# Feed-forward input of a hybrid decoder trunk: combinations of weight blocks made by adding DMAs

## The chip, the cores and the metric

The kernel runs on one core of one Trainium2 chip. The metric is the device time of one execution in microseconds (us); the median of three runs of the kernel before is 1497.92 us (1497.32 to 1499.15).

## What is computed

The reference is one layer of a decoder trunk for 256 tokens with a width of 2048, all in float32: three parallel token mixers with gates and an output projection, then a cross attention into 256 memory tokens, then a SwiGLU feed-forward. The change touches only the first half of the feed-forward:

```python
h = rms_norm(x, ffn_pre_gain[l])
gt, up = jnp.split(h @ w_ffn_in[l], 2, axis=-1)        # w_ffn_in: 2048 x 11264, FFN_HIDDEN = 5632
x = x + rms_norm((jax.nn.silu(gt) * up) @ w_ffn_out[l], ffn_post_gain[l])
```

## The kernel before, in words

**Weights in units.** All weights are streamed from HBM in units of 512 KB: 128 partitions x 1024 float32, that is two tiles of 128 x 512. A queue of the sync engine (SP in the profile) loads them into `raw`, a ring of four buffers. Every product is made of float32 numbers split into two parts: ScalarE (ACT) copies a unit into `w_hi` in the reduced type (line 547 in the feed-forward), VectorE (DVE) subtracts it from `raw` to give `w_lo` (line 995), and TensorE (PE) multiplies hi by hi, lo by hi and hi by lo. `w_hi` and `w_lo` are rings of four too. This pair of operations on one unit is called a split here. The split for step v waits for `unit_used >= v - 3`, that is until PE has finished step v - 4; it starts when PE begins step v - 3.

**Bodies.** The feed-forward input has 11 column groups of 512 gate columns (left, G) and 512 up columns (right, U). The first group is computed plainly. The other ten are ten bodies of 19 steps each, i = 1 to 10. In a body 12 steps are plain units (12 matmuls of 128 x 512 each), six for G and six for U. The remaining quarter of the sum is done by a Strassen-like scheme with seven block products (6 matmuls each) where a plain computation has eight. It takes a 2 x 2 arrangement of weight units B11, B12 (gate and up of one half of the rows) and B21, B22, and the same of the inputs. The weight sides of the seven products are, in this order, B11, B12 - B11, B22 - B12, B22 - B12 + B11, B22, B21 and B21 - (B22 - B12 + B11); the left-hand sides are sums of input blocks, `S_f`, formed once (`x_sums`, line 1600). The partial products go to the PSUM banks `side[2]`, `side[3]`, `tr[0]` and `tr[1]`, and DVE folds them into the two column groups afterwards (`sum_p6`, `sums_p7_p5`, `sum_p5`, `gate_sum`, `up_sum`).

**Who forms the combinations of weight blocks.** DVE does, in `difference` (line 1003): four subtractions per body, in place in `raw`, before the split of the combination. In the program the order of a body is fixed: six plain units, the seven block products one behind another, six plain units. Steps are numbered r0 to r18 below, and the four subtractions make the combinations of r7, r8, r9 and r12.

**The order on the other engines.** Everything is written out by hand. A Python function, `late_units`, makes the list of loads (which unit into which of the four buffers, and after how many splits that buffer is free) and the list of steps. SP walks the loads in order, each behind a wait for `lo_ready`, the count of finished splits. ACT and DVE walk the same steps four ahead of PE; at position j of body i they do the split of step j + 4 of that body. Between the splits stand the other tasks of the body, at fixed positions: on DVE `up_sum` and `hidden_product` of the body before (j = 0, 1), `hidden_turn` (j = 2, two 32 x 32 block transposes into `h_blk`), the partial sums (j = 13 to 16) and `hidden_lo` (j = 17); on ACT the copy of one partial product out of PSUM (line 928), `hidden_hi` (line 595) and Silu (line 934). GpSimd (POOL) issues 16 small DMAs of 32 KB per body (`spread_blocks`, line 502) once the transposes are done; they finish the transposition of the hidden activations, and `hidden_hi` waits for their landing.

The same scheme occurs six times in the second half of the feed-forward (`out_pair`); it keeps the DVE subtractions.

Of the kernel before, what the change touches and what calls it, by code (L numbers as in the profile page):

```python
# [40 lines left out]
RING = 4  # L41
# [23 lines left out]


def late_units():

    loads, steps = [], {}
    free, rounds = [S_FI - 3 + k for k in range(RING)], [S_FI // RING] * RING  # L70
    slot, pairs = 0, 0

    def load():
        nonlocal slot
        s, slot = slot, (slot + 1) % RING
        rounds[s] += 1
        loads.append((S_FI + len(loads), s, free[s]))
        return s, rounds[s] * 16

    def plain(count):  # L80
        for _ in range(count):
            s, landed = load()
            v = S_FI + len(steps)
            steps[v] = ("plain", 0, 0, (s,), (landed,))
            free[s] = v + 1

    def pair():
        nonlocal slot, pairs
        v = S_FI + len(steps)
        slots, landed = zip(*[load() for _ in range(4)])  # L90
        for k in range(7):
            steps[v + k] = ("pair", k, pairs, slots, landed)
        for s, done in zip(slots, (7, 3, 5, 6)):
            free[s] = v + done
        slot, pairs = (slot + 1) % RING, pairs + 1

    for _ in range(10):
        plain(6)
        pair()
        plain(6)  # L100
# [8 lines left out]
    assert len(steps) == S_END - S_FI  # L109
    return loads, steps  # L110


LATE_LOADS, LATE_STEPS = late_units()
B11, B12, B22, B21 = range(4)

# [41 lines left out]
def trunk(nc, units, x, x_t, mem, mem_t, columns, gm_ws_t, s5_b_t, s5_c_t, gm_v_gain,  # L157
          mix_post_gain, xattn_post_gain, ffn_post_gain, out):
    with ExitStack() as ctx:
# [138 lines left out]
        def bank(b, h):  # L298
# [44 lines left out]
        t_ready, p1_copied, u_part, u_done, silu_ready, hb_ready = (  # L343
            sem("t_ready"), sem("p1_copied"), sem("u_part"), sem("u_done"), sem("silu_ready"), sem("hb_ready"))
        hs_ready, hs_hi, hs_lo = sem("hs_ready"), sem("hs_hi"), sem("hs_lo")
        hT_turned, hT_hi_ready, hT_ready = sem("hT_turned"), sem("hT_hi_ready"), sem("hT_ready")
# [62 lines left out]
        def _(pool):  # L409
# [103 lines left out]
        def _(act):  # L513
# [22 lines left out]
            def split_late(v):  # L536

                if v >= S_END:
                    return
                kind, k, n, slots, landed = LATE_STEPS[v]  # L540
                block = 0 if kind == "plain" else (B11, B11, B12, B11, B22, B21, B11)[k]
                if kind == "plain" or k in (0, 4, 5):
# [377 lines left out]
            def ffn_in(i):  # L920
                for j in range(FI_SPLITS):
                    if j == 12:
                        act.wait_ge(unit_used, body_base(i) + 7)
                        if i == 1:
                            act.wait_ge(acc_taken[1], G_FI + 2)
                        else:
                            act.wait_ge(hb_ready, i - 1)
                        a_.activation(silu_g[:, 0], side[:, 2], ACT.Copy).then_inc(p1_copied, 1)
                    if j == 15:
                        hidden_hi(i)  # L930
                    if j == 17:
# [47 lines left out]
        def _(dve):  # L979
# [25 lines left out]
            def split_late(v):  # L1005
# [3 lines left out]
                kind, k, n, slots, landed = LATE_STEPS[v]  # L1009
                if kind == "plain":  # L1010
                    split_at(slots[0], v)
                    return
# [587 lines left out]
            def x_sums():  # L1600

                a = [[xg[:, h, 0].rearrange("p (q e) t -> p e q t", e=2)[:, e] for e in range(2)] for h in range(HALVES)]
                own.link(v_.tensor_tensor(S_f[:, 0], a[1][0], a[1][1], ALU.add))
                own.link(v_.tensor_tensor(S_f[:, 1], S_f[:, 0], a[0][0], ALU.subtract))
                v_.tensor_tensor(S_f[:, 2], a[0][0], a[1][0], ALU.subtract)
                v_.tensor_tensor(S_f[:, 3], a[0][1], S_f[:, 1], ALU.subtract).then_inc(s_ready, 1)

# [23 lines left out]
            def up_sum(i, h):  # L1631

                if h == 0:
                    dve.wait_ge(acc0_full, G_FI + 2 + i)
                else:
                    dve.wait_ge(unit_used, body_base(i + 1))
                v_.tensor_tensor(hb[:, h], bank(1, h), hb[:, h], ALU.add).then_inc(acc_taken[h], 1)

# [8 lines left out]
            def gate_sum(i, h):  # L1647

                dve.wait_ge(unit_used, body_base(i) + 12 + h)
# [8 lines left out]

            def sums_p7_p5(m, second, third):
# [4 lines left out]
                v_.tensor_tensor(second, side[:, 3], second, ALU.add).then_inc(u_part, 1)  # L1664

            def sum_p5(m, third, fourth):

                dve.wait_ge(u_part, 3 * m)
                v_.tensor_tensor(fourth, side[:, 3], third, ALU.add).then_inc(u_done, 1)

            def ffn_in(i):
                for j in range(FI_SPLITS):
# [10 lines left out]
                    if j == 2:  # L1683
                        hidden_turn(i)
                    if j == 13:
                        dve.wait_ge(unit_used, body_base(i) + 10)
                        dve.wait_ge(h_blocked, i)
                        sum_p6(i, silu_g[:, 0], hb[:, 0])
                    if j == 14:
                        sums_p7_p5(i, hb[:, 0], silu_g[:, 1])  # L1690
                    if j == 15:
                        sum_p5(i, silu_g[:, 1], hb[:, 1])
                        gate_sum(i, 0)
                    if j == 16:
                        gate_sum(i, 1)
                    if j == 17:
# [92 lines left out]
        def _(pe):  # L1789
# [307 lines left out]

            def pair_products(v, hi, lo, g, s_hi_, s_lo_, x12_free, first, last):
# [5 lines left out]
                if x12_free is not None:  # L2104
                    pe.wait_ge(acc_taken[0], x12_free)
                pair_product(v + 4, side[:, 0], *sum_of(s_hi_, s_lo_, 3), x12_free is not None, False)
                pair_product(v + 5, acc[:, 0], *block_of(hi, lo, g, 1, 0), False, x12_free is not None)
                pair_product(v + 6, acc[:, 1], *block_of(hi, lo, g, 1, 1), False, x12_free is not None)

# [35 lines left out]
            def out_pair(q, k, pair):  # L2145

                pe.wait_ge(hs_lo, k + 1)
                pe.wait_ge(u_done, 10 + pair)
                pair_products(S_FO + q, hT_hi, hT_lo, k, H_hi[k], H_lo[k], None, k == 0, k == PAIRED - 1)

# [119 lines left out]
```

## Time and profile before

| | |
|---|---|
| median of three runs | 1497.92 us |
| the profiled execution's own time | 1497.17 us |
| its span, first to last instruction | 1495.1 us |
| PE (TensorE) busy | 1483.7 us, 99% |
| DVE (VectorE) busy | 1129.9 us, 76% |
| ACT (ScalarE) busy | 825.7 us, 55% |
| POOL (GpSimd) busy | 151.9 us, 10% |
| mean granted TensorE clock | 0.998 |
| moved by DMA | 305.08 MB |
| ten bodies of the feed-forward input | from 834.06 us on, 42.16 us each |

The span is the time on the core's engines; the execution's own time has 2.1 us more around it. A busy engine is one with an instruction in flight. Matmul rows overlap: a row of 0.39 us stands every 0.227 us. The idle time of an engine costs something only where PE waits for it in turn.

### The profile page before, as it was taken

How to read it: one execution, taken by the hardware profiler on the slowest of the kernel's cores; microseconds unless marked ns; L12 is line 12 of the kernel's file. 1: busy time of each engine (PE TensorE's matmuls, PEld its weight loads, DVE VectorE, ACT ScalarE, POOL GpSimd, SP SyncE). 2: the span in 40 equal slices, each digit the busy share in tenths (PEclk: the TensorE clock that was granted, in tenths of full speed). 3: DMA queues.
4: the chain of work that ended last, by engine and by line, in shares of the span. 5: the costliest groups of instructions: out<-in, count | busy, mean ns of one | idle time of the engine just before them, and what ended most of it. 6: DMA issues, size and time to landing. Idle time of an engine off the chain costs nothing.

```text
span 1495.1 us, 19180 instructions
## 1 busy us (share of the span) xinstructions
PE 1483.7 (99%) x6718; PEld 1221.6 (82%) x6718; DVE 1129.9 (76%) x1346; ACT 825.7 (55%) x990; POOL 151.9 (10%) x286
## 2 busy tenths in 40 slices
PE   9999999999999999999999999999999999999997
PEld 7888887888888888888887888888888888888886
DVE  7878988855554577557577788888888888887786
ACT  7645445565666444556576455555555555555553
POOL 0000000140220000000000221112222221000000
PEclk9999999999999999999999999999999999999999
DMA  9755555666565655856453666766666667657554
GB/s 347 234 187 179 172 183 181 200 197 197 186 194 172 237 181 186 325 195 212 155 197 113 199 209 221 230 212 214 209 210 203 202 214 233 231 171 238 197 184 154
DMA packets 89858, 305.08 MB, mean 204 GB/s; under 512 B 13056, under 2 KB 13568, under 8 KB 88768
## 3 DMA queue, kind: packets, MB, share of 16 engines
q1 hardware_dynamic: 80144, 285.12, 57.4%
q0 software_dynamic: 9216, 18.63, 3.9%
q8 instruction: 41, 0.67, 0.2%
q10 hardware_dynamic: 432, 0.45, 0.1%
q14 instruction: 25, 0.20, 0.0%
HBM read 294.19 MB, written 2.10 MB: 198 GB/s over the span
## 4 chain that ended last, share of the span: by engine, by line
PE 97%; DVE 1%; DMA 1%; ACT 1%; issue 0%; DVEq 0%; POOL 0%; SPq 0%; ACTq 0%; POOLq 0%
PE acc L1803 10%; PE acc L1805 9%; PE acc L1804 9%; PE acc L2123 6%; PE acc L2124 6%; PE acc L2121 6%; PE side L2123 5%; PE side L2124 5%; PE side L2121 5%; PE side L1803 3%; PE side L1804 3%; PE side L1805 3%; PE tr L1805 3%; PE tr L1803 3%; PE tr L1804 3%; PE side L2085 1%
## 5 line engine op out<-in xcount | busy, mean ns | idle before, releaser
L547 ACT ACTIVATE w_hi<-raw 128x1024 fp32r<-128x1024 f32 x296 | 312.5, 1061 | 300.6 <-PE acc L2124 98.6
L990 DVE TENSOR_TENSOR w_lo<-raw,w_hi 128x1024 fp32r<-128x1024 f32 x262 | 320.9, 1227 | 202.0 <-ACT w_hi L528 197.7
L995 DVE TENSOR_TENSOR w_lo<-raw,w_hi 128x1024 fp32r<-128x1024 f32 x312 | 378.6, 1223 | 113.8 <-ACT w_hi L547 103.0
L528 ACT ACTIVATE w_hi<-raw 128x1024 fp32r<-128x1024 f32 x262 | 277.1, 1060 | 281.0 <-PE acc L1805 165.8
L1803 PE MATMUL acc<-w_hi,xT_hi 128*128 128x512 f32 x504 | 198.2, 393 | 0.0
L1805 PE MATMUL acc<-w_hi,xT_lo 128*128 128x512 f32 x504 | 196.3, 389 | 0.0
L1804 PE MATMUL acc<-w_lo,xT_hi 128*128 128x512 f32 x504 | 196.3, 389 | 0.0
L502 POOL DMA_DIRECT2D hT_st<-h_blk x176 | 93.9, 542 | 493.7 <-DVE h_blk L1062 455.3
L1803 PEld LDWEIGHTS acc<-w_hi,xT_hi 128*128 128x128 f32 x504 | 94.6, 188 | 21.5 <-issue 1.6
L1805 PEld LDWEIGHTS acc<-w_hi,xT_lo 128*128 128x128 f32 x504 | 94.6, 188 | 20.0
L1804 PEld LDWEIGHTS acc<-w_lo,xT_hi 128*128 128x128 f32 x504 | 94.7, 188 | 19.1
L2121 PE MATMUL acc<-w_hi,xT_hi 128*128 128x512 f32 x240 | 93.4, 389 | 0.0
L2123 PE MATMUL acc<-w_lo,xT_hi 128*128 128x512 f32 x240 | 93.4, 389 | 0.0
L2124 PE MATMUL acc<-w_hi,xT_lo 128*128 128x512 f32 x240 | 93.4, 389 | 0.0
L2121 PE MATMUL side<-w_hi,xT_hi 128*128 128x512 f32 x240 | 93.4, 389 | 0.0
L2123 PE MATMUL side<-w_lo,xT_hi 128*128 128x512 f32 x240 | 93.4, 389 | 0.0
L2124 PE MATMUL side<-w_hi,xT_lo 128*128 128x512 f32 x240 | 93.4, 389 | 0.0
L1003 DVE TENSOR_TENSOR raw<-raw 128x1024 f32<-128x1024 f32 x64 | 78.3, 1224 | 3.3 <-DMA raw<-in_units 0.6
L1803 PE MATMUL tr<-w_hi,xT_hi 128*128 128x512 f32 x192 | 75.8, 395 | 0.0
L1805 PE MATMUL tr<-w_hi,xT_lo 128*128 128x512 f32 x192 | 74.9, 390 | 0.0
L1804 PE MATMUL tr<-w_lo,xT_hi 128*128 128x512 f32 x192 | 74.8, 390 | 0.0
L1803 PE MATMUL side<-w_hi,xT_hi 128*128 128x512 f32 x160 | 62.7, 392 | 0.5 <-DVE w_lo L990 0.5
(467 smaller groups left out, 2743.2 us busy)
## 6 DMA issues: line engine op xcount, KB each, us to landing
raw<-in_units SPq DMA_DIRECT2D x530, 512.0 KB, 4.2
hT_st<-h_blk POOLq DMA_DIRECT2D x176, 32.0 KB, 2.1
x_tok<-in_x SPq DMA_DIRECT2D x4, 512.0 KB, 5.9
qkT<-qk_blk POOLq DMA_DIRECT2D x64, 32.0 KB, 2.6
xres<-in_x POOLq DMA_DIRECT2D x1, 2048.0 KB, 10.4
m_raw<-in_mem_t POOLq DMA_DIRECT2D x1, 2048.0 KB, 10.9
mq<-in_mem POOLq DMA_DIRECT2D x1, 2048.0 KB, 17.7
x_raw<-in_x_t SPq DMA_DIRECT2D x6, 256.0 KB, 5.9
```

The costliest lines, as they stand in the source:

```text
L502: g.dma_start(hT_st[32 * a:32 * a + 32, :, b].rearrange("p h k c -> p h (k c)"), h_blk[32 * b:32 * b + 32, :, a].rearrange("p h k c -> p h ...
L528: a_.activation(w_hi[:, j % RING], raw[:, j % RING], ACT.Copy).then_inc(hi_ready, 1)
L547: a_.activation(w_hi[:, v % RING], raw[:, slots[block]], ACT.Copy).then_inc(hi_ready, 1)
L990: v_.tensor_tensor(w_lo[:, s], raw[:, s], w_hi[:, s].bitcast(F32), ALU.subtract).then_inc(lo_ready, 1)
L995: v_.tensor_tensor(lo[:, v % RING], raw[:, slot], hi[:, v % RING].bitcast(F32), ALU.subtract).then_inc(lo_ready, 1)
L1003: v_.tensor_tensor(raw[:, dst], raw[:, minuend], raw[:, subtrahend], ALU.subtract).then_inc(t_ready, 1)
L1803: pe.matmul(bank(b, h), hi[:, kt, tok], w_hi[:, s, k], start=begin, stop=False)
L1804: pe.matmul(bank(b, h), hi[:, kt, tok], w_lo[:, s, k], start=False, stop=False)
L1805: mm = pe.matmul(bank(b, h), lo[:, kt, tok], w_hi[:, s, k], start=False, stop=end)
L2121: pe.matmul(bank(b, h), hi[:, kt, tok], whi[:, k], start=(j == 0 and k == 0 and begins[h] is not None), stop=False)
L2123: pe.matmul(bank(b, h), hi[:, kt, tok], wlo[:, k], start=False, stop=False)
L2124: mm = pe.matmul(bank(b, h), lo[:, kt, tok], whi[:, k], start=False, stop=(last and j == count - 1 and k == 1))
```

## The change

The four combinations of a body are no longer made by DVE. GpSimd issues DMAs that read a unit from HBM and add it to what lies in a buffer of `raw` (`accum_op=ALU.add`), four per body. Since a DMA adds only, the signs are moved: the inputs' block sums and the folding on DVE take other signs (`x_sums`, `up_sum`, `sums_p7_p5`, `sum_p5`), so that the weights' combinations are B22 + B12, B11 + B12, B22 + B12 + B11 and B22 + B12 + B11 + B21. B12 is no longer loaded by itself; it is read twice, by two adding DMAs. A body has 15 loads and 4 adding DMAs where it had 16 loads.

The order of the 19 steps changes: the seven products no longer stand together. Their steps are r2 (B22), r3 (B11), r6, r7, r10 (sums), r13 (B21) and r14 (sum), and in every case a DMA fills or adds to a buffer right behind the split four steps ahead of its next use. The number of matmuls is the same. The wait of PE for `u_done` of the body before and for the bank that the up columns leave (`acc_taken[0]`) move to r2; the latter stood ahead of r10 before.

```diff
+BODY = ("G0", "G1", "B22", "B11", "G2", "G3", "B22+B12", "B11+B12", "G4", "G5", "B22+B12+B11",
+        "U0", "U1", "B21", "B22+B12+B11+B21", "U2", "U3", "U4", "U5")
+SUMS = ("B22+B12", "B11+B12", "B22+B12+B11", "B22+B12+B11+B21")
...
+    def body(i):
+        nonlocal v, u
+        at = {}
+        for r, what in enumerate(BODY):
+            if "+" in what:
+                held, added = what.rsplit("+", 1)
+                slot, split = at[held]
+                sums.append((SUMS.index(what), slot, u + BODY_UNITS.index(added), split + 1))
+                steps[v + r] = ("sum", SUMS.index(what), i, (slot,), (16 * i,))
+            else:
+                longer = [k for k, w in enumerate(BODY) if w == what or w.startswith(what + "+")]
+                slot, landed = load(u + BODY_UNITS.index(what), v + longer[-1] + 1)
+                steps[v + r] = ("plain", 0, 0, (slot,), (landed,))
+            at[what] = slot, v + r
...
-            spread_blocks(1)
-            for i in range(2, 12):
+            def add_blocks(role, slot, u, splits):
+
+                pool.wait_ge(lo_ready, splits)
+                g.dma_start(raw[:, slot].rearrange("p a b -> p (a b)"), units[u], accum_op=ALU.add).then_inc(sum_landed[role], 16)
+
+            for i in range(1, 11):
+                for k in range(3):
+                    add_blocks(*LATE_SUMS[4 * (i - 1) + k])
                 spread_blocks(i)
+                add_blocks(*LATE_SUMS[4 * (i - 1) + 3])
+            spread_blocks(11)
...
+                if kind == "sum":
+                    act.wait_ge(sum_landed[k], landed[0])
...
-                    if j == 12:
-                        act.wait_ge(unit_used, body_base(i) + 7)
+                    if j == 5:
+                        act.wait_ge(unit_used, body_base(i) + 4)
...
-                    if j == 15:
+                    if j == 14:
                         hidden_hi(i)
...
             for i in range(1, 11):
                 v, taken = body_base(i), i * 2 + G_FI
-                plain_units(v, 6, 0, xT_hi, xT_lo, 4, (taken - 1, taken - 1))
+                plain_units(v, 2, 0, xT_hi, xT_lo, 4, (taken - 1, taken - 1))
                 if i == 1:
                     pe.wait_ge(s_lo, 1)
                 else:
                     pe.wait_ge(u_done, i - 1)
-                pair_products(v + 6, xT_hi, xT_lo, 0, S_hi, S_lo, taken, True, True)
-                plain_units(v + 13, 6, 1, xT_hi, xT_lo, 4, (None, taken), True)
+                pe.wait_ge(acc_taken[0], taken)
+                pair_product(v + 2, side[:, 0], *sum_of(S_hi, S_lo, 3), True, False)
+                pair_product(v + 3, side[:, 2], *block_of(xT_hi, xT_lo, 0, 0, 0), True, True)
+                plain_units(v + 4, 2, 0, xT_hi, xT_lo, 8)
+                pair_product(v + 6, tr[:, 0], *sum_of(S_hi, S_lo, 2), True, True)
+                pair_product(v + 7, side[:, 3], *sum_of(S_hi, S_lo, 0), True, True)
+                plain_units(v + 8, 2, 0, xT_hi, xT_lo, 12)
+                pair_product(v + 10, tr[:, 1], *sum_of(S_hi, S_lo, 1), True, True)
+                plain_units(v + 11, 2, 1, xT_hi, xT_lo, 4, (None, taken))
+                pair_product(v + 13, acc[:, 0], *block_of(xT_hi, xT_lo, 0, 1, 0), False, True)
+                pair_product(v + 14, acc[:, 1], *block_of(xT_hi, xT_lo, 0, 1, 1), False, True)
+                plain_units(v + 15, 4, 1, xT_hi, xT_lo, 8, last=True)
```

**GpSimd's queue.** The order on GpSimd from the start of the bodies, before. `hT_st<-h_blk` are the 16 small DMAs of a body.

```order
L494 DMA post_gain<-in_xattn_post_gain 128x2048 [waits acc1_taken,acc0_taken]
L502 DMA hT_st<-h_blk 32x2x128 [waits h_blocked]
L502 DMA hT_st<-h_blk 32x2x128 x15
L502 DMA hT_st<-h_blk 32x2x128 [waits hT_ready,h_blocked]
L502 DMA hT_st<-h_blk 32x2x128 x15
```

And the same place now; `raw<-in_units` is an adding DMA.

```order
L512 DMA post_gain<-in_xattn_post_gain 128x2048 [waits acc1_taken,acc0_taken]
L526 DMA raw<-in_units 128x1024 [waits lo_ready] x3
L520 DMA hT_st<-h_blk 32x2x128 [waits h_blocked]
L520 DMA hT_st<-h_blk 32x2x128 x15
L526 DMA raw<-in_units 128x1024 [waits lo_ready] x4
L520 DMA hT_st<-h_blk 32x2x128 [waits hT_ready,h_blocked]
L520 DMA hT_st<-h_blk 32x2x128 x15
```

Three adding DMAs stand ahead of the small DMAs of a body and the fourth behind them; the row of four is the fourth of body 1 and the first three of body 2.

**VectorE in a body.** The order on DVE in body 1 before, from the transposes of `hidden_turn` to the second of the partial sums. `w_lo<-raw,w_hi` is the DVE half of a split, `raw<-raw` a subtraction of weight blocks.

```order
L1062 STREAM_TRANSPOSE h_blk<-hb 128x4x4x32 x2
L995 TENSOR_TENSOR w_lo<-raw,w_hi 128x1024
L1003 TENSOR_TENSOR raw<-raw 128x1024 x2
L995 TENSOR_TENSOR w_lo<-raw,w_hi 128x1024
L1003 TENSOR_TENSOR raw<-raw 128x1024
L995 TENSOR_TENSOR w_lo<-raw,w_hi 128x1024 x3
L1003 TENSOR_TENSOR raw<-raw 128x1024
L995 TENSOR_TENSOR w_lo<-raw,w_hi 128x1024 x6
L1657 TENSOR_TENSOR hb<-tr,silu_g 128x512
L995 TENSOR_TENSOR w_lo<-raw,w_hi 128x1024
L1662 TENSOR_TENSOR silu_g<-tr,hb 128x512
```

And now:

```order
L1090 STREAM_TRANSPOSE h_blk<-hb 128x4x4x32 x2
L1023 TENSOR_TENSOR w_lo<-raw,w_hi 128x1024 x9
L1685 TENSOR_TENSOR hb<-tr,silu_g 128x512
L1023 TENSOR_TENSOR w_lo<-raw,w_hi 128x1024
L1690 TENSOR_TENSOR silu_g<-tr,hb 128x512
L1692 TENSOR_TENSOR hb<-hb,side 128x512
L1023 TENSOR_TENSOR w_lo<-raw,w_hi 128x1024
L1697 TENSOR_TENSOR hb<-silu_g,side 128x512
```

The four subtractions are gone. The partial sums begin two splits earlier: the first (`hb<-tr,silu_g`) stands between the splits of r14 and r15.

**ScalarE in a body.** The ACT halves of the splits from r6 on, in body 1, now; `sum_landed` is the landing of an adding DMA.

```order
L575 ACTIVATE w_hi<-raw 128x1024 [waits unit_used,sum_landed0]
L575 ACTIVATE w_hi<-raw 128x1024 [waits unit_used,sum_landed1]
L575 ACTIVATE w_hi<-raw 128x1024 [waits unit_used,w_landed0]
L956 ACTIVATE silu_g<-side 128x512 [waits acc1_taken,unit_used]
L575 ACTIVATE w_hi<-raw 128x1024 [waits unit_used,w_landed1]
L575 ACTIVATE w_hi<-raw 128x1024 [waits unit_used,sum_landed2]
L575 ACTIVATE w_hi<-raw 128x1024 [waits unit_used,w_landed3]
```

Before, the splits of combinations (r7, r8, r9 and r12) waited there for DVE's count `t_ready`; now those of r6, r7, r10 and r14 wait for a DMA.

## Rows read from the trace of the kernel before

**Rows 1.** The page: busy time, share of the span, instructions of two engines.

```profile
PE 1483.7 (99%) x6718; PEld 1221.6 (82%) x6718; DVE 1129.9 (76%) x1346; ACT 825.7 (55%) x990; POOL 151.9 (10%) x286
```

**Rows 2.** Waits of PE: who waited for whom, us in total, times, longest.

```profile
PE acc L2039 <- DVE xT_lo L1543: 1.4, 2, 1.3
PE side L1826 <- POOL warm L412: 1.4, 1, 1.4
PE side L1803 <- DVE w_lo L990: 0.5, 1, 0.5
```

**Rows 3.** Windows, one per body: length, busy us (x instructions), clock, DMA share.

```profile
core 0: us, PE busy (x) PEld busy (x) DVE busy (x) ACT busy (x) POOL busy (x), PEclk, DMA share, GB/s
876.22:918.38 42.16, 42.16 (x187) 34.91 (x186) 35.84 (x36) 22.74 (x23) 8.53 (x16) 1.00 0.66 208
918.38:960.54 42.16, 42.16 (x188) 34.91 (x186) 35.94 (x36) 22.74 (x23) 8.54 (x16) 1.00 0.70 218
```

**Rows 4.** Timeline of PE, body 3: start us, us, then what it is.

```profile
934.70 0.39 PE L2084 MATMUL side<-w_hi,xT_hi 128*128 128x512 f32 x1
...
936.06 0.39 PE L2084 MATMUL side<-w_hi,S_hi 128*128 128x512 f32 x1
...
944.22 0.39 PE L2121 MATMUL side<-w_hi,xT_hi 128*128 128x512 f32 x1
...
960.54 0.39 PE L2121 MATMUL acc<-w_hi,xT_hi 128*128 128x512 f32 x1
```

**Rows 5.** The subtractions of weight blocks in 886 to 1264 us: min/median/max ns.

```profile
L1003 DVE TENSOR_TENSOR raw<-raw x36: 1217/1225/1227, 887.0 to 1233.7; 128x1024 f32<-128x1024 f32 x36
```

**Rows 6.** Timeline of ACT at the start of body 4 (960.54 us).

```profile
960.80 1.06 ACT L547 ACTIVATE w_hi<-raw 128x1024 fp32r<-128x1024 f32 x1 [1.66 <-PE side L2124]
```

**Rows 7.** Timeline of DVE in bodies 3 and 4.

```profile
948.94 0.69 DVE L1657 TENSOR_TENSOR hb<-tr,silu_g 128x512 f32<-128x512 f32 x1
...
961.89 1.23 DVE L995 TENSOR_TENSOR w_lo<-raw,w_hi 128x1024 fp32r<-128x1024 f32 x1 [1.49 <-ACT w_hi L547]
963.03 1.28 DVE L1637 TENSOR_TENSOR hb<-side,hb 128x512 f32<-128x512 f32 x2
...
968.48 1.30 DVE L1062 STREAM_TRANSPOSE h_blk<-hb 128x512 f32<-128x512 f32 x2
970.05 1.22 DVE L995 TENSOR_TENSOR w_lo<-raw,w_hi 128x1024 fp32r<-128x1024 f32 x1 [0.28 <-ACT w_hi L547]
```

**Rows 8.** Timeline of DVE ahead of and in body 1 (starts at 834.06 us).

```profile
823.97 1.22 DVE L1611 TENSOR_TENSOR S_lo<-S_f,S_hi 128x1024 fp32r<-128x1024 f32 x1
...
836.55 1.40 DVE L1618 SCALAR_TENSOR_TENSOR hb<-side,rstd,silu_g 128x512 f32<-128x512 f32 x2
```

**Rows 9.** Timeline of POOL: the 16 small DMAs of bodies 2 and 3.

```profile
885.75 8.53 POOL L502 DMA_DIRECT2D hT_st<-h_blk  x16 [33.59 <-DVE h_blk L1062]
927.91 8.54 POOL L502 DMA_DIRECT2D hT_st<-h_blk  x16 [33.63 <-DVE h_blk L1062]
```

**Rows 10.** Timeline of POOL: issue of two DMAs of 512 KB.

```profile
33.83 0.69 POOL L429 DMA_DIRECT2D B_all<-in_s_b_t  x1 [30.67 <-DMA x_tok<-in_x]
34.52 0.53 POOL L430 DMA_DIRECT2D C_all<-in_s_c_t  x1
```

**Rows 11.** DMA queues in 886 to 1264 us: packets, MB, share of 16 engines.

```profile
q1 hardware_dynamic: 20690, 75.32, 60.5%
q0 software_dynamic: 4608, 4.73, 4.8%
raw<-in_units SPq DMA_DIRECT2D x144, 512.0 KB, 4.3
```

**Rows 12.** Unit loads in 886 to 1264 us, then small DMAs: landing, min/median/max.

```profile
DMA to landing us min/median/max: 3.0/4.3/6.5
...
DMA to landing us min/median/max: 1.7/2.1/4.9
```

**Rows 13.** DMA issues of GpSimd, whole kernel: count, KB, median us to landing.

```profile
post_gain<-in_xattn_post_gain POOLq DMA_DIRECT2D x1, 1024.0 KB, 7.0
post_gain<-in_ffn_post_gain POOLq DMA_DIRECT2D x1, 1024.0 KB, 7.6
B_all<-in_s_b_t POOLq DMA_DIRECT2D x1, 512.0 KB, 5.5
C_all<-in_s_c_t POOLq DMA_DIRECT2D x1, 512.0 KB, 7.7
```

More of the change, by code:

```diff
@@ L73, in load @@
-    def load():
-        nonlocal slot
-        s, slot = slot, (slot + 1) % RING
+    v, u, pairs = S_FI, S_FI, 0
+    def load(unit, done):
+        s = free.index(min(free))
         rounds[s] += 1
-        loads.append((S_FI + len(loads), s, free[s]))
+        loads.append((unit, s, free[s]))
+        free[s] = done
         return s, rounds[s] * 16
     def plain(count):
+        nonlocal v, u
         for _ in range(count):
-            s, landed = load()
-            v = S_FI + len(steps)
+            s, landed = load(u, v + 1)
@@ L84, in plain @@
             steps[v] = ("plain", 0, 0, (s,), (landed,))
-            free[s] = v + 1
+            v, u = v + 1, u + 1
     def pair():
-        nonlocal slot, pairs
-        v = S_FI + len(steps)
-        slots, landed = zip(*[load() for _ in range(4)])
+        nonlocal v, u, pairs
+        slots, landed = zip(*[load(u + k, v + done) for k, done in enumerate((7, 3, 5, 6))])
         for k in range(7):
             steps[v + k] = ("pair", k, pairs, slots, landed)
-        for s, done in zip(slots, (7, 3, 5, 6)):
-            free[s] = v + done
@@ L95, in pair @@
[L95 to L100, printed above, removed]
+        v, u, pairs = v + 7, u + 4, pairs + 1
+    def body(i):
+        nonlocal v, u
+        at = {}
[10 more added lines that the diff above has]
+            at[what] = slot, v + r
+        v, u = v + len(BODY), u + len(BODY_UNITS)
@@ L101, in late_units @@
+    for i in range(1, 11):
+        body(i)
     for count in (12, 8, 4):
@@ L108, in late_units @@
     plain(12)
-    assert len(steps) == S_END - S_FI
-    return loads, steps
-LATE_LOADS, LATE_STEPS = late_units()
+    assert v == S_END
+    return loads, steps, sums
+LATE_LOADS, LATE_STEPS, LATE_SUMS = late_units()
 B11, B12, B22, B21 = range(4)
@@ L344, in trunk @@
             sem("t_ready"), sem("p1_copied"), sem("u_part"), sem("u_done"), sem("silu_ready"), sem("hb_ready"))
+        sum_landed = [sem(f"sum_landed{i}") for i in range(4)]
         hs_ready, hs_hi, hs_lo = sem("hs_ready"), sem("hs_hi"), sem("hs_lo")
@@ L540, in split_late @@
                 kind, k, n, slots, landed = LATE_STEPS[v]
-                block = 0 if kind == "plain" else (B11, B11, B12, B11, B22, B21, B11)[k]
-                if kind == "plain" or k in (0, 4, 5):
+                block = 0 if kind != "pair" else (B11, B11, B12, B11, B22, B21, B11)[k]
+                if kind == "sum":
+                    act.wait_ge(sum_landed[k], landed[0])
+                elif kind == "plain" or k in (0, 4, 5):
                     act.wait_ge(w_landed[slots[block]], landed[block])
@@ L1009, in split_late @@
                 kind, k, n, slots, landed = LATE_STEPS[v]
-                if kind == "plain":
+                if kind != "pair":
                     split_at(slots[0], v)
@@ L1636, in up_sum @@
                     dve.wait_ge(unit_used, body_base(i + 1))
-                v_.tensor_tensor(hb[:, h], bank(1, h), hb[:, h], ALU.add).then_inc(acc_taken[h], 1)
+                v_.tensor_tensor(hb[:, h], bank(1, h), hb[:, h], ALU.subtract).then_inc(acc_taken[h], 1)
             def hidden_product(i):
@@ L1647, in gate_sum @@
             def gate_sum(i, h):
-                dve.wait_ge(unit_used, body_base(i) + 12 + h)
+                dve.wait_ge(unit_used, body_base(i) + 14 + h)
                 if h == 1:
@@ L1657, in sum_p6, with sums_p7_p5 @@
                 v_.tensor_tensor(second, tr[:, 1], first, ALU.add).then_inc(u_part, 1)
-            def sums_p7_p5(m, second, third):
+            def sums_p7_p5(m, second, third, op=ALU.add):
                 dve.wait_ge(u_part, 3 * m - 2)
@@ L1663, in sums_p7_p5, with sum_p5 @@
                 dve.wait_ge(u_part, 3 * m - 1)
-                v_.tensor_tensor(second, side[:, 3], second, ALU.add).then_inc(u_part, 1)
-            def sum_p5(m, third, fourth):
+                v_.tensor_tensor(second, second, side[:, 3], op).then_inc(u_part, 1)
+            def sum_p5(m, third, fourth, op=ALU.add):
                 dve.wait_ge(u_part, 3 * m)
-                v_.tensor_tensor(fourth, side[:, 3], third, ALU.add).then_inc(u_done, 1)
+                v_.tensor_tensor(fourth, third, side[:, 3], op).then_inc(u_done, 1)
             def ffn_in(i):
@@ L2096, in sum_of, with pair_products @@
                 return (lambda q: hi[:, m, q]), (lambda q: lo[:, m, q])
-            def pair_products(v, hi, lo, g, s_hi_, s_lo_, x12_free, first, last):
+            def pair_products(v, hi, lo, g, s_hi_, s_lo_, first, last):
                 pair_product(v, side[:, 2], *block_of(hi, lo, g, 0, 0), first, last)
```

38 lines of the change are left out of this document (18 added, 20 removed).

## The prediction, made before the changed kernel was run

> **What bounds the kernel now.** I read four views, from the whole to one body. The page first: PE has an instruction in flight for 1483.7 of 1495.1 us [rows 1]. Then the waits of PE: three in the whole kernel, 3.3 us together, and none of them on a weight combination [rows 2]. Then windows cut at the bodies: 42.16 us each, PE busy for all of it at a granted clock of 1.00 (the level of 2.4 GHz), DVE for 35.9 us, GpSimd for 8.5 us [rows 3]. Last the timeline of PE in body 3: from the first block product at 934.70 us to the next plain unit at 944.22 us are 42 matmuls, 9.52 us or 0.2267 us each; the product of 6 takes 936.06 - 934.70 = 1.36 us [rows 4]. A body has 12 x 12 + 7 x 6 = 186 matmuls, and 186 x 0.2267 = 42.16 us, the window's length to the last digit. So nothing is lost in a body: PE issues at its pace through the subtractions of DVE, and whatever ACT, DVE and the DMAs do lies beside it.
>
> **What the change removes.** Four subtractions of 1.225 us per body [rows 5], 4.9 us, 49 us over ten bodies. By the above they are hidden in full: worth 0 us. DVE's idle time in a body grows from 6.3 to about 11 us. The matmuls are as many as before and in the same shapes, so a body can't be shorter than 42.16 us. The change can only add waits, and the question is whether the adding DMAs are in time.
>
> **The timetable.** In us from the start of a body, with 2.72 for a plain unit and 1.36 for a product, the new steps start on PE at: r0 0, r1 2.72, r2 5.44, r3 6.80, r4 8.16, r5 10.88, r6 13.60, r7 14.96, r8 16.32, r9 19.04, r10 21.76, r11 23.12, r12 25.84, r13 28.56, r14 29.92, r15 31.28, r16 34.00, r17 36.72, r18 39.44, next body 42.16. A split starts when PE begins the step three earlier: ACT at 960.80 for a body that begins at 960.54, +0.26 [rows 6]; DVE begins at 961.89 and its result is there at 963.12, +2.6 [rows 7]. From a landing to the end of the split that waited for it are about 1.0 + 1.3 = 2.3 us. D is the time of an adding DMA from its issue to its landing.
>
> - r2 to r6: the split of r2 is done at -0.1. The add for r6 must be there by 13.60 - 2.3 = 11.3: D up to 11.4.
> - r3 to r7: issued at 2.6, needed by 12.7: D up to 10.
> - r6 to r10: its split comes behind the transposes on DVE, which end at 969.78, or 9.3 into the body, and the split of one more unit ends at 971.27, or 10.7 [rows 7]. Needed by 19.5: D up to 8.8.
> - r10 to r14: here GpSimd's order counts. The third add is issued at 10.7 and holds GpSimd for 0.5 to 0.7 us [rows 10]; the 16 small DMAs behind it take 8.54 us [rows 9]; so the fourth add, whose split would be ready at 17.6, is issued only at 19.9. DVE has the first partial sum (0.69 us [rows 7]) between the splits of r14 and r15, so r14's split has to be done by 31.28 - 0.7 - 1.2 = 29.4. D up to 29.4 - 2.3 - 19.9 = 7.2. This is the tightest place.
>
> Beyond these single limits there is a loop from body to body, in which each of three adds waits for the one before: from PE's start of r15 to that of r18 8.16, the split of the next r2 2.6, three times D + 2.3, the partial sum and the split of r15 1.9; together 19.6 + 3 D, against 42.16: D up to 7.5. So below some 7.2 us an add costs nothing, and above about 7.4 each us of D costs 3 us per body, 30 us in all.
>
> **How long is an adding DMA?** The trace has none; it is bounded by its neighbours. From below: a plain load of a unit lands after 4.3 us in the median, 3.0 at the least [rows 12]. From above: a DMA that GpSimd issues with twice the bytes takes 7.0 and 7.6 us, and the second of two 512 KB DMAs at once 7.7 us [rows 13]. I take 5.9: the fixed part by a small DMA of GpSimd, 2.1 [rows 12], then the transfer. 144 loads took 60.5% of 378 us, 1.6 us of all 16 engines each [rows 11]; an add has two streams of 512 KB to read, the unit and the buffer, so I take twice that, 3.2. A load needs 0.6 us more in the median than 2.1 + 1.6, for what shares the engines with it, and I give the add the same. That is 1.3 us under the tightest limit, so no wait: 0 us.
>
> The Trainium skill bears on the factor of two (Collectives: The Full Stack, "The bandwidth ceiling: the fold count and why AG ≠ RS ≠ AR"): the add inside a DMA costs nothing by itself, but the two source reads go through one ring and halve the rate, 32.35 against 62.28 GB/s. No row here shows it. By that page an add would be an estimated 1.93 x 1.6 = 3.1 us of transfer; by a plain copy's rate it would be 1.6. Both keep the sum at 0 us.
>
> **The DMA engines and the ring.** Per body 15 loads x 1.6 = 24.0, four adds x 3.2 = 12.8, small DMAs 4.8% of 42.16 = 2.0 us: 38.8 of 42.16, or 92%, where it was 65%. The order helps: behind each split exactly one DMA starts, a load or an add, so they come one after the other every 1.36 to 2.72 us and don't bunch. Each buffer's content is used four steps after the DMA began; 19 steps of 42.16 us allow 8.9 us per four steps, less the split's 2.3: all DMAs together may take 6.6 us in the mean. With loads at 4.3 and adds at 5.9 the mean is 4.6; with loads at 6 it would still hold.
>
> **The moved waits.** PE now waits at r2 for the bank that `up_sum` frees: DVE does its first half by 963.7, 3.2 into the body [rows 7], and r2 starts at 5.44; 2.2 us to spare. In body 1 that is the product at 836.55 plus 0.7, or 3.2 into it, as much to spare; and `S_lo` is there at 825.2, r2 starts at 839.5 [rows 8]. The small DMAs start 1.9 us later (11.4 instead of 9.5) and land at about 22; `hidden_hi` wants them at 31.5, the split behind which it stands. No cost. GpSimd has 4 x 0.6 us more to issue, in 33.6 us of idle time [rows 9]. Outside the ten bodies nothing moves.
>
> **The sum.** The profiled execution's own time is 1497.17 us, 2.1 more than its span, and 0.75 below the median of the runs. Minus 0, plus 0: the changed kernel takes the median's 1497.92, rounded 1498.0.
>
> **The rivals.**
> 1. *The adding DMA is slower than 7.4 us, and each body waits for it* (slower). For it: the same bytes from GpSimd took 7.7 us once, in company [rows 13]; the rate of an add is shown nowhere; three of four adds hang on one another, so a small excess is tripled. Against: 7.7 was the second of two issued together, here they come singly, except after r2 and r3. At 7.7 us it is 3 x 0.3 x 10 = 9 us, 1507; at 8.5 us 3 x 1.1 x 10 = 33 us, 1531. It decides from 7.4 us on. PE would wait at r14 and r15, for a split behind `sum_landed3`. Chance 24%.
> 2. *The DMA engines fill up* (slower). The adds take more of the engines than two streams, or the loads beside them stretch past the ring's 6.6 us. If loads and adds take 7.2 in the mean, 19/4 x 0.6 = 2.9 us per body, 29 in all, 1527. For it: 92% is close to full, and single loads take 6.5 already [rows 12]. Against: the spacing. Chance 12%.
> 3. *Faster by more than 0.2%.* It would need a loss in the bodies that the trace of before doesn't show. PE's waits there are zero and its pace doesn't depend on DVE's load. Chance 4%.
> 4. No change, the forecast: 60%.
>
> **How the numbers follow.** 0.2% (3 us) is what a measurement of this kernel can tell from no change. Within it lies the forecast, 60%; the likeliest case's own range is 1495 to 1501. Slower: rivals 1 and 2, 36%. Faster: 4%. The range goes up to 1531, where both slower cases as priced end; the tail above it, an add of over 8.5 us, holds some 15%. Below it ends at 1495.
>
> **What would show it.** Right: bodies of 42.16 us in the windows, no wait of PE on `w_lo` in them; ACT's copies for r6 and r10 start later than PE lets them, since the adds land after that (for r10 the slack without any shift is 15.2 - 10.7 = 4.5 us, less than D), and still PE doesn't wait; DVE at about 31 us per body. Adds of 5 to 7 us, loads of 4.3 to 5.5. Wrong: bodies over 42.5 us with PE waiting for DVE's split at r14 or r15 and ACT for a DMA before it (rival 1); or ACT waiting for plain loads and DMA engines over 90% busy (rival 2).

## The result, and the profile after

The changed kernel takes 1508.93 us (median of 4 runs, 1504.47 to 1511.67) against 1497.81 us: a ratio of 1.0073, 95% interval 1.0061 to 1.0084. It is slower by 11 us. The forecast of no change, given 60%, was wrong. The range held the time, but by the room it left for the rivals and not by the sum. The first rival, given 24%, comes nearest: PE waits at r14 for a split behind an adding DMA that is slower than 7.4 us. But only the fourth add of a body is slow, and not every body waits. The profiled execution took 1511.67 us; its span is 1509.9 us, 14.8 longer than before.

First the page's line of the engines, which answers to [rows 1], and the waits of PE, which answer to [rows 2] (who waited for whom, us in total, times, longest).

```profile
PE 1490.6 (99%) x6718; PEld 1222.5 (81%) x6718; DVE 1081.3 (72%) x1306; ACT 824.3 (55%) x990; POOL 187.7 (12%) x326
...
PE acc L2111 <- DVE w_lo L1023: 6.6, 5, 3.1
```

DVE has 49 us less to do, as worked out; PE has as many matmuls and is busy 7 us longer. A wait has appeared that is not in [rows 2]: the product on `acc` (r14) waits for DVE's half of a split. Windows cut at PE's start of r14 in one body and the next answer to [rows 3]; the columns are those of [rows 3].

```profile
864.22:907.62 43.40, 42.81 (x187) 34.76 (x186) 31.09 (x33) 22.51 (x24) 12.11 (x20) 1.00 0.85 242
907.62:952.70 45.08, 42.81 (x186) 34.77 (x187) 31.09 (x33) 22.40 (x24) 12.12 (x20) 1.00 0.83 233
952.70:996.71 44.01, 44.01 (x187) 35.98 (x187) 31.10 (x33) 22.03 (x23) 12.10 (x20) 0.96 0.85 239
996.71:1039.80 43.09, 43.01 (x189) 35.32 (x189) 32.12 (x34) 23.82 (x25) 12.12 (x20) 1.00 0.85 245
```

These four are 43.1 to 45.1 us long, where a body took 42.16. In the third window PE never idles and still takes 44.01 us, at a mean granted clock of 0.96. Cut at r0 instead, the ten bodies take 42.2 to 47.2 us; here are bodies 3, 5 and 7. Bodies 3 and 7 lose 9.1 us together, the other eight 5.4.

```profile
920.41:966.68 46.27, 44.06 (x188) 35.98 (x187) 31.84 (x33) 22.38 (x23) 12.12 (x20) 0.96 0.83 237
1009.45:1051.62 42.17, 42.17 (x187) 34.88 (x186) 31.20 (x33) 22.74 (x23) 12.12 (x20) 1.00 0.88 250
1094.04:1141.21 47.17, 44.06 (x187) 35.97 (x186) 31.85 (x33) 22.50 (x23) 12.13 (x20) 0.96 0.82 229
```

The chain of waits through body 3 shows the cause (start us, us, what), and the timeline of PE behind it shows the price.

```profile
931.05 0.84 POOL raw L526
931.89 6.46 POOL hT_st L520 x12
938.36 0.91 issue
939.26 2.13 POOL hT_st L520 x4
941.39 8.91 DMA raw<-in_units
950.31 0.02 issue
950.33 1.07 ACT w_hi L575
951.40 0.02 issue
951.42 1.24 DVE w_lo L1023
952.66 0.04 issue
952.70 0.50 PE acc L2111
```

```profile
952.70 0.50 PE L2111 MATMUL acc<-w_hi,xT_hi 128*128 128x512 f32 x1 [2.21 <-DVE w_lo L1023]
...
954.44 0.63 PE L2113 MATMUL acc<-w_hi,xT_lo 128*128 128x512 f32 x1
954.87 0.63 PE L2146 MATMUL side<-w_hi,xT_hi 128*128 128x512 f32 x1
955.29 0.63 PE L2148 MATMUL side<-w_lo,xT_hi 128*128 128x512 f32 x1
...
957.13 0.39 PE L2146 MATMUL side<-w_hi,xT_hi 128*128 128x512 f32 x1
```

Read the chain from the bottom: PE waits for the split of r14, the split for the fourth add, the add for GpSimd, which was busy with the small DMAs of `hT_st` and stood still for 0.91 us amid them. After the idle 2.2 us the matmuls stand 0.43 us apart instead of 0.227 (0.63 us each instead of 0.39), the pace of the 1.2 GHz level, and are back at the other level by 956.9. From 952.70 to 957.00 the granted clock is 0.60 in the mean. A wait of 2.2 us thus cost about 4.1. Over the ten bodies, what the distances between the starts of matmuls have over 0.227 us (where that is 0.08 us or more) adds up to 14.1 us, nearly the 14.8 of the span.

### The profile page after: what moved, and what is told of

The parts are those of the page before. It is cut to its first block, busy times and chain, and to the rows that moved or that the text cites. A ratio compares the mean times of both kernels' runs of the same rounds, so it can differ in the third digit from the quotient of the medians.

```text
span 1509.9 us, 19120 instructions
## 1 busy us (share of the span) xinstructions
PE 1490.6 (99%) x6718; PEld 1222.5 (81%) x6718; DVE 1081.3 (72%) x1306; ACT 824.3 (55%) x990; POOL 187.7 (12%) x326
## 4 chain that ended last, share of the span: by engine, by line
PE 82%; POOL 5%; DMA 5%; issue 4%; DVE 3%; ACT 2%; SPq 0%; DVEq 0%; ACTq 0%; POOLq 0%
PE acc L1830 10%; PE acc L1832 10%; PE acc L1831 10%; DMA raw<-in_units 5%; PE side L2146 4%; PE side L2148 4%; PE side L2149 4%; POOL hT_st L520 4%; PE side L1830 4%; PE side L1831 3%; PE side L1832 3%; PE acc L2146 3%; PE acc L2148 3%; PE acc L2149 3%; PE tr L1832 3%
## 5 line engine op out<-in xcount | busy, mean ns | idle before, releaser
L526 POOL DMA_DIRECT2D raw<-in_units x40 | 37.0, 926 | 436.7 <-DVE w_lo L1023 436.7
```

What stands on the lines that cost most here:

```text
L526: g.dma_start(raw[:, slot].rearrange("p a b -> p (a b)"), units[u], accum_op=ALU.add).then_inc(sum_landed[role], 16)
```

## The experiments

Two words for the texts below: theory A is GpSimd's order (the fourth add is late), rival B the filling of the DMA engines. "The limit" is 27.1 us into the body, by which the fourth add must have landed by the prediction. Places in a body are counted from PE's start of its r0, in each kernel's own trace. Each ratio is to the kernel before on the same chip. Its median there was 1497.43 us for the first four runs and 1497.75 for the eleven fills, VectorE's work spread and the changed kernel again; for the other four it was 1497.99.

**The fourth add ahead of the small DMAs.**

```diff
             for i in range(1, 11):
-                for k in range(3):
+                for k in range(4):
                     add_blocks(*LATE_SUMS[4 * (i - 1) + k])
                 spread_blocks(i)
-                add_blocks(*LATE_SUMS[4 * (i - 1) + 3])
```

> The fourth adding DMA of a body is issued ahead of the 16 small DMAs, nothing else. Theory A (order of GpSimd's queue: the small DMAs both hold the fourth add back to 20.0 us into the body and lie ahead of it on the way to the engines, so it takes 7.2 to 8.9 us where the other three take 5.3 to 7.7): it is issued at about 17.7, lands in 5.3 to 7 us, by about 24; no wait of PE in the bodies, bodies of 42.16 us, 1497 to 1500 us. Rival B (the DMA engines are full, 85% busy, and every add and load is stretched): the traffic is the same, the waits stay, 1504 to 1512.

Measured: 1498.97 us, ratio 1.0017 (1.0007 to 1.0026), no wait of PE in the bodies. Timeline of POOL (start us, us, what) in body 1 of the changed kernel, then of this one:

```profile
845.48 8.85 POOL L520 DMA_DIRECT2D hT_st<-h_blk  x16
854.08 1.22 POOL L526 DMA_DIRECT2D raw<-in_units  x1
```

```profile
853.03 0.84 POOL L526 DMA_DIRECT2D raw<-in_units  x1 [7.38 <-DVE w_lo L1022]
853.60 8.86 POOL L520 DMA_DIRECT2D hT_st<-h_blk  x16
```

In body 1 the issue moves by about 1 us only, from 19.8 to 18.9 into the body and not to 17.7, since the split of r10 is not done sooner; but the add now lands after 5.2 to 6.5 us in all ten bodies, where it took 7.2 to 8.9. Order alone brings back 10 of the 11 us. Theory A holds, B fails. The two halves of theory A are not told apart by this run. An estimate from these rows: issued at 19.8 with the others' 5.9 us it would land at 25.7, issued at 18.9 with its own 7.75 us at 26.7, both under the limit of 27.1. In body 7, where GpSimd pauses for 2.8 us amid the small DMAs in both kernels, only the order helps: there the fourth add of the changed kernel was issued at 23.0. What is left is at the end: the small DMAs, now later, make PE wait 0.7 us for the last hidden block (row below), and `hidden_hi` delays the splits behind it, so the first two adds come 1.1 to 2.7 us apart. Where they are 1.1 to 1.2 apart, the second takes 8.4 to 8.9 us; where it is 2.7, 5.2 to 6.1.

```profile
PE acc L2145 <- DVE hT_lo L1097: 0.7, 1, 0.7
```

**Half ahead, half behind.** `spread_blocks(i, range(2))` ahead of the fourth add, `spread_blocks(i, range(2, 4))` behind it.

> Eight of the 16 small DMAs stay ahead of the fourth add, eight go behind it. Theory A: they end at about 15.7 into the body, before the split that the add waits for (17.6), so it is issued at 17.7; it lands in 6 to 7 us, by about 24.5; no wait of PE, 1497 to 1500. Rival B: 1504 to 1512, as before this edit.

Measured: 1498.40 us, ratio 1.0009 (0.9999 to 1.0018): not told from the kernel before. The fourth add is issued at 18.5 to 20.0, not at 17.7, and takes 5.2 to 7.7 us. No wait of PE is listed in the bodies; cut at r0, they are 0.6 us over 421.6 in all, 0.45 of it in body 2, where the add landed at 27.5. Windows over all ten bodies, the kernel before, then this one:

```profile
834.06:1255.66 421.60, 421.60 (x1862) 349.10 (x1860) 358.39 (x358) 227.18 (x230) 85.38 (x160) 1.00 0.66 212
```

```profile
834.06:1255.66 421.60, 421.51 (x1859) 348.50 (x1858) 310.63 (x318) 226.63 (x230) 121.84 (x200) 1.00 0.89 249
```

PE is at its pace, but for these 0.6 us, with the DMA engines at 0.89 instead of 0.66.

**Plain copies in place of the adds.** `accum_op=ALU.add` is left out, so the sums of weight blocks are not formed.

> The four adding DMAs of a body are plain copies of the same unit into the same buffer (the sums of weight blocks are left out), issued at the same places. If an add's transfer takes twice a copy's (two streams read): the first three go from a median near 5.7 to 4.2 to 4.6 us, the fourth from 7.7 to about 6.2 and lands at 26.2, under the limit of 27.1, so PE's waits go, 1497 to 1500. If the adding itself costs nothing and the time is the queue's and the fixed part's: times to landing as with the adds, 1504 to 1512.

Measured: 1497.76 us, ratio 1.0003 (0.9994 to 1.0013). The first three of a body land after 3.8 us in the median (21 of 30 after 3.5 to 3.9), the fourth, right behind the small DMAs, after 4.4 to 6.1 (median 5.1). Issue on GpSimd (min/median/max ns), of this kernel and of the changed one, then the software queue's share of the engines in 886 to 1264 us, in the same order:

```profile
L526 POOL DMA_DIRECT2D raw<-in_units x40: 531/536/583, 834.3 to 1233.9; - x40
...
q0 software_dynamic: 9504, 22.56, 19.1%
```

```profile
L526 POOL DMA_DIRECT2D raw<-in_units x40: 835/858/1225, 834.4 to 1246.6; - x40
...
q0 software_dynamic: 9504, 22.56, 31.6%
```

With the same bytes booked, 34 adds take 12.5% of 378 us more: 1.4 us each on top of a copy's 1.6, and the first three land 1.9 us later in the median. That is nearly the factor of two that I chose. It agrees with the factor that the Trainium skill gives (Collectives: The Full Stack, "The bandwidth ceiling: the fold count and why AG ≠ RS ≠ AR"); the reason given there, two source reads through one ring, no run here shows. The expected time and the end of PE's waits are met; the copies land sooner than expected, 3.8 us against 4.2 to 4.6 and 5.1 against about 6.2. So an add costs more over a copy than the doubled transfer alone: 1.9 us to landing for 1.4 us of the engines.

**Scratch fills in place of the small DMAs.** The small DMAs go behind the fourth add; 13 `memset` of 128 x 512 stand ahead of it.

> The 16 small DMAs go behind the fourth add, and in their place ahead of it GpSimd fills a scratch area 13 times (7 to 9 us, no DMA). So the add is issued as late as in the changed kernel, about 20, with nothing of the small DMAs ahead of it in the queue. Theory A with the backlog as what counts: it lands in 5.3 to 6.5 us, by 26.5, no wait or one under 0.3 us, 1497 to 1501. Theory A with the late issue as what counts (and the fourth add slow for another reason): waits stay, 1504 to 1512. Rival B: 1504 to 1512 with loads and first adds as slow as before.

Measured: 1501.87 us, ratio 1.0029 (1.0019 to 1.0039). GpSimd's rows in body 6:

```profile
1060.07 7.86 POOL L533 MEMSET pad<- 128x512 f32 x13
1068.22 0.83 POOL L527 DMA_DIRECT2D raw<-in_units  x1 [0.30 <-POOL pad L533]
```

The fills end sooner than the small DMAs did: the add is issued at 19.3 in six bodies (19.8 in the changed kernel), so the run doesn't copy the late issue in full. The fourth add takes 5.3 to 5.5 us in three bodies and 7.1 to 8.3 in seven, with no small DMA ahead of it. So neither of my two readings was right: the backlog is not needed for a slow add. I compared its issue with SyncE's next load. In the seven slow cases that load began 0.3 to 0.62 us after the add (six) or 1.23 (one); in the three fast ones 0.93 to 1.39 after. In the kernel with the add first, the load always began 0.86 us or more after it, and the add took 6.5 at most.

**Eleven fills.**

> As the run with 13 scratch fills ahead of the fourth add, with 11: the add is issued 1.2 us earlier, at about 18.1 into the body, 1 us ahead of the load behind the split of r11 (19.0) and not beside it. If the add's 7.1 to 8.3 us there came from meeting that load: 5.3 to 6.2 us here, landing by 24.3, no waits, 1498 to 1500. If an add ahead of which small DMAs or fills stand is slow for another reason: 7 us and more in several bodies again, 1500 to 1502.

Measured: 1499.67 us, ratio 1.0016 (1.0005 to 1.0026). The add was not issued at 18.1 but at 18.9 to 20.6 (19.2 in body 1, 853.70, with GpSimd idle for 1.3 us ahead of it): the split of r10 held it, not the fills. So the run didn't put the add clear of the load, and doesn't decide as it was meant to. With the load 0.61 or 0.62 us behind it the add took 7.1, 8.3, 7.1 and 7.2; with the load 1.11 us or more behind, 5.4 or 5.5 in four bodies, but 7.0 and 8.0 in two. Over the three kernels, add first, 13 fills and 11 fills, a load that began within 0.65 us behind went with an add of over 7 us in 10 of 10 cases, a later load with one of 7.0 us or more in 3 of 20. Two of the three waits of PE in this kernel, 2.3 of 3.3 us, are not on the fourth add at all but at r7, behind a second add that followed the first by 1.14 us and took 10.5 and 9.6 us.

**The delay of the third add.** In the kernel with the add first, fills stand ahead of the third add.

```diff
                 for k in range(4):
+                    if k == 2:
+                        pool.wait_ge(lo_ready, LATE_SUMS[4 * (i - 1) + 2][3])
+                        for _ in range(2):        # 6 in the second kernel
+                            own.link(g.memset(pad[:], 0.0))
                     add_blocks(*LATE_SUMS[4 * (i - 1) + k])
```

> The fourth add ahead of the small DMAs, and GpSimd fills a scratch area twice (1.2 us) ahead of the third add. By the limits (third add issued at 12.0 instead of 10.8, landing by 17.6, needed by 19.5; fourth landing by about 25.5, needed by 27.1) nothing comes of it: within 2 us of 1499.0. If adds are so close to the limit that any delay is paid: 10 x 1.2 = 12 us more, 1511.

> The same with six fills (3.6 us) ahead of the third add. By the limits the third add is issued at 14.4 and lands at about 20, 0.5 over its limit, and the fourth, issued at 22.3, lands at about 28, 0.9 over: PE waits 0.5 to 1.5 us per body, in all or nearly all bodies, with TensorE's slower pace after the longer waits on top: 1504 to 1516. If the limits are wrong and there is slack: 1499.

Measured: two fills 1505.86 us, ratio 1.0047 (1.0031 to 1.0064); six fills 1542.26 us, 1.0298 (1.0268 to 1.0328). Both were expected lower, and in both the third add is the first thing that the limits had wrong. They gave it 5.6 us wherever it was issued. But the fills also move it towards SyncE's loads:

```profile
1179.16 0.84 POOL L527 DMA_DIRECT2D raw<-in_units  x1 [0.30 <-POOL pad L534]
1180.25 0.33 SPq L419 DMA_DIRECT2D raw<-in_units  x1
DMA to landing us min/median/max: 5.3/5.3/5.3
```

```profile
1222.64 0.84 POOL L527 DMA_DIRECT2D raw<-in_units  x1 [0.30 <-POOL pad L534]
1222.88 0.33 SPq L419 DMA_DIRECT2D raw<-in_units  x1
DMA to landing us min/median/max: 8.6/8.6/8.6
```

These are the third add of bodies 8 and 9 with six fills, SyncE's next load, and the add's time to landing. With six fills, nine third adds begin 0.14 to 0.66 us before or behind a load and take 7.4 to 9.3 us, the tenth (body 8) takes 5.3; with two fills, three begin 0.04 to 0.31 us from a load and take 7.2 to 8.5, seven 2.0 us or more from one and take 5.1 to 5.5. In all eleven profiles with adds together, 30 of 440 adds began within 0.66 us of a load of SyncE's queue, before or behind, and each of them took 7.1 us or more; of the other 410, 65 took 7.0 or more, and their median is 5.7. So an add that comes within 0.66 us of a load is slow, wherever the fills or the order put it there. How the one slows the other is not shown, and a load moved by itself was not tried.

There is more. With two fills the small DMAs, moved on by them, land too late for `hidden_hi`, which stands in ACT's queue ahead of splits (first row below, ACT's waits; 15.6 us in the kernel with the add first); the next body's first two adds are then issued 1.14 us apart, in seven bodies (three in the kernel with the add first), and the second takes 8.4 to 9.4 us there. With six fills PE waits 2.1 to 4.8 us for r10 in the nine bodies whose third add was slow (second row), and not in the tenth. From two to six fills 2.4 us of delay per body cost 3.6: more than itself. The slow third adds are one part of it; the slower pace, which follows five of the nine waits and costs 1.7 to 2.7 us each time, is another. It does not follow the other four, of 2.2 to 3.1 us: the windows behind a wait of 2.48, one of 2.24 and one of 3.10 us, with granted clocks of 0.58, 1.00 and 1.00, stand below the waits.

```profile
ACT hT_hi L627 <- DMA hT_st<-h_blk: 17.2, 10, 4.0
PE tr L2115 <- DVE w_lo L1027: 28.0, 9, 4.8
...
904.01:908.01 4.00, 4.00 (x11) 3.13 (x12) 3.35 (x3) 1.53 (x2) 3.76 (x7) 0.58 0.58 98
950.33:954.33 4.00, 4.00 (x17) 3.30 (x18) 3.35 (x3) 1.53 (x2) 3.77 (x7) 1.00 0.60 92
1141.51:1145.51 4.00, 4.00 (x18) 3.31 (x19) 3.35 (x3) 1.54 (x2) 3.04 (x5) 1.00 0.55 74
```

**More traffic.** 37 further loads of 256 KB from SyncE's queue into a scratch area, in the half-and-half kernel.

> The half-and-half kernel with 37 more loads of 256 KB from SyncE's queue into a scratch area, one behind every fourth load of the bodies: 3.7 per body, 0.8 us of the 16 engines each, 3 us per body, so the engines go from about 88% to 95% busy. Rival B (the engines are what binds): PE waits appear, 1502 to 1515. Theory A (what counts is when the adds are issued and what lies next to them): loads and adds land 0.3 to 1 us later, within 2 us of 1498.4.

Measured: 1499.16 us, ratio 1.0013 (1.0004 to 1.0023), 0.8 over the half-and-half kernel's median. Windows over the bodies:

```profile
834.06:1255.66 421.60, 421.36 (x1855) 347.38 (x1854) 309.64 (x317) 225.81 (x230) 121.92 (x200) 1.00 0.94 271
```

The engines are busy 0.94 of the time, and no wait of PE is listed in the bodies. PE does not quite keep its pace: cut at r0 the bodies are 1.6 us over 421.6, 1.0 more than in the half-and-half kernel, all of it in bodies 1, 5 and 8, whose third add took 7.9 to 8.0 us and whose fourth landed at 27.2 to 27.5. Loads land after 5.4 us in the median, adds after 6.3. Rival B is out as the cause of the 11 us: a fuller set of engines than the changed kernel's (0.86 over its bodies) costs about 1 us.

**VectorE's work given back.** Eight operations of 128 x 512 per body into a scratch area, in the half-and-half kernel: first at positions 3 (four), 4 and 7 (two each), where the subtractions had been; then two each at 8, 9, 10 and 18.

> The half-and-half kernel with the work of the four removed subtractions given back to VectorE: eight operations of 128 x 512 into a scratch area per body, at positions 3, 4 and 7. If VectorE's relief is worth nothing (theory A: PE had no wait to lose): within 1 us of the half-and-half kernel's 1498.4, no wait of PE in the bodies. If the relief is what lets the late adds be caught up (a rival, C): waits of PE return and it takes 1501 or more.

> The half-and-half kernel with the same eight VectorE operations per body as the run that gave the work back at positions 3, 4 and 7 (1506.5), now two each at positions 8, 9, 10 and 18, where VectorE has idle time ahead of splits. If only the place decided: within 1.5 us of 1498.4, no wait at r8. If the amount of VectorE work decides: 1503 to 1508 again.

Measured: 1506.52 us, ratio 1.0057 (1.0040 to 1.0073), and 1501.76 us, 1.0026 (1.0014 to 1.0037). Waits of PE in the first:

```profile
PE acc L2152 <- DVE w_lo L1025: 5.8, 10, 0.9
```

PE waits at r8 in each of ten bodies, for a split behind the six extra operations. These take more than was removed:

```profile
L1718 DVE TENSOR_TENSOR pad<-xres x80: 677/691/696, 844.3 to 1242.8; 128x512 f32<-128x512 f32 x80
```

Eight of 0.69 us are 5.5 us per body against 4.9, and the six ahead of r8's split 4.1 against 3.7, a surplus of about 0.45 us. PE's wait there is 0.54 or 0.55 us in nine bodies, which are at least 0.85 us longer than 42.16, so about half of the loss may be the surplus; what an equal amount of work would have cost is open. Spread over idle places the loss halves: against the kernel before on each chip it is 8.5 and 4.0 us, and 1.0 for the half-and-half kernel. It doesn't go away: in five bodies the third add takes 7.4 to 8.1 us; what slows it there was not followed up. So the place counts, and my expectation that this order has room for all of the work at no cost was wrong for the work as it was given back; that the amount counts too is likely, not shown.

**The changed kernel again**, on the chip of the runs with eleven fills and with VectorE's work spread.

> The changed kernel itself once more, on the same chip as the two runs beside it: 1504 to 1512, waits of PE at r14 and r15, the fourth add at 7.2 to 8.9 us.

Measured: 1508.02 us, ratio 1.0064 (1.0047 to 1.0081), with the fourth add at 6.3 to 9.1 us and four waits of PE at r14, 6.2 us together, none at r15. The time holds. Again the longest wait, 4.3 us, is in body 7, where GpSimd paused for 2.8 us amid the small DMAs.

## What of the prediction was right and what was wrong, point by point

- *Nothing to gain in the bodies.* Right. No kernel of the study was faster than the one before, and the three that list no wait of PE in the ten bodies or right behind them, half-and-half, plain copies and more traffic, were within 0.15% of it.
- *The first adds, D = 5.9.* Right in size: 5.3 to 7.7 us, medians 5.5, 6.1 and 5.9 for the first, second and third. Twice a copy's transfer was right within 0.2 us.
- *The fourth add.* Here the sum failed. The step "issued only at 19.9" was right (19.8 in eight bodies, 21.0 and 23.0 in bodies 3 and 7), and so was the limit: in body 5 the add landed at 27.0 and nothing was lost, in body 6 at 27.25 and 0.25 us were. But I gave this add the 5.9 of the others. It took 7.2 to 8.9, median 7.75, and landed at 27.8 in the median, 29.9 and 30.8 in bodies 3 and 7. I held the 7.7 us of [rows 13] against an add in company, and called the adds single except after r2 and r3. That left out two kinds of company. All ten fourth adds are issued right behind the 16 small DMAs, the last of them 0.5 us ahead; a plain copy in that place took 5.1 us in the median against 3.8. And four of the ten begin within 0.66 us of a load of SyncE's. The other six, 0.68 to 1.54 us from one, took 7.2 to 8.4 as well, so the loads alone don't explain the changed kernel. How much each kind adds was not taken apart.
- *Rival 1's price.* At 7.7 us it was 9 us, and 11 were measured. That is luck: the 9 are three late adds per body in a loop, 3 x 0.3 us in each of ten bodies. The other three adds were never late and the loop never closed; what was measured comes of one late add, and over half of it of the two bodies with a pause of GpSimd.
- *"Whose split would be ready at 17.6".* Wrong: that left out the third add's own landing, at 16.5, and the 2.3 us of the split behind it. With the add first it is issued at 18.9 in body 1, so the order costs this add only about 1 us of issue, and yet 2 us of landing.
- *The small terms.* An add holds GpSimd for 0.86 us in the median, not 0.5 to 0.7, and the 16 small DMAs take 8.85 us. In bodies 3 and 7 GpSimd stood still for 0.91 and 2.80 us amid the small DMAs. These bodies have the two longest waits of PE, 2.2 and 3.1 us, and with the slower pace make 9.1 of the 14.5 us that the ten bodies lost in the profiled execution. Such gaps are in the trace of before too (1.47 and 0.23 us, in bodies 4 and 5), where nothing hung on them. The sum had no term for them.
- *The price of a wait.* I left out that PE can go on at the slower level after a wait of over 2 us: here after both such waits, 1.7 us more each.
- *The relief is worth 0.* True against the kernel before, whose order had room for the subtractions; for the new order it is open how much of it is needed: work of 5.5 us per body, 0.6 more than was removed, cost 7.6 us over the half-and-half kernel in the old places and 3.0 spread out.
- *The engines, the ring, the moved waits.* The engines were estimated at 92% and are at 82 to 88% by body; they don't bind. PE's new wait at r2 never showed.

## What to carry to other kernels

A DMA whose landing is waited for should stand ahead of a batch of small DMAs on its queue, or amid them, if the batch can wait; here that was worth 10 of 11 us. An adding DMA costs its engines about twice a copy (3.0 against 1.6 us) and keeps GpSimd longer (0.86 against 0.54 us), so it needs its own place in the spacing of all DMAs, the other queue's too. A DMA's time to landing is not one number: price it at each place by what is issued beside it. When work is moved off an engine that nobody waits for, count only what the new chain can lose: a kernel with PE at 100% in the stage can't win by it.

## What the runs showed of the hardware

- Two adding DMAs of 512 KB 1.1 to 1.2 us apart: the second lands after 8.4 to 10.5 us; 2.7 us apart: 5.2 to 6.4. Plain copies from the same queue: 3.5 to 3.9 in 21 of the 30 that have no small DMAs right ahead.
- An adding DMA that began within 0.66 us of a 512 KB load of SyncE's queue, before or behind, took 7.1 to 9.3 us, in 30 of 30 cases in eleven profiles; the median of the other 410 adds is 5.7.
- The small DMAs of 32 KB landed after 2.1 us in the median before, 4.1 with plain copies ahead of them, 5.8 with adds.
- In the changed kernel PE ran some nine matmuls at 0.43 us each after idle stretches of 2.2 and 3.1 us, at a granted clock of 0.57 and 0.60 over the 4.0 and 4.3 us behind, and at full pace after those of 0.5 us and less. With six fills it was so after five of nine stretches of 2.1 to 4.8 us (2.15, 2.48, 3.54, 4.50 and 4.78), and not after 2.24, 2.58, 2.59 and 3.10: the length of the stretch alone does not decide.
- GpSimd's issue of DMAs can pause, here by 0.2 to 2.8 us in single bodies; in body 7 of all twelve profiles with the new order it was 2.6 to 2.8 us. In the changed kernel's longest pause lies one packet of an instruction queue; whether that is the cause was not tried.
